# Gate rows leave from a copy turned by TensorE, and the out projection's first weight chunk is split inside the scan's last step

## The chip, the cores and the metric

The kernel runs on one core of one Trainium2 chip. The metric is the device time of one execution in microseconds (us), lower being better. PE is TensorE, DVE is VectorE, ACT is ScalarE, POOL is GpSimd, and SP is SyncE, which here only issues DMAs.

## The reference, cut to what matters

The program computes two blocks one after the other, each two layers deep, on 256 tokens of width 1024, all in float32. The second block works on two streams, the latent tokens (`lat`) and the context tokens (`ctx`). Its layer 0 is what the change touches:

```python
ml = jnp.split(s_lat @ w_ada[i] + b_ada[i], 6, axis=-1)      # shift, scale, gate of the mixer, and of the ff
mc = jnp.split(s_ctx @ w_ada[i] + b_ada[i], 6, axis=-1)
u_lat = modulate(h_lat, g_pre_mix[i], ml[0], ml[1])
...
# even_mixer: the first 512 columns come from an RWKV-7 scan in both directions, the other 512 from attention
out_lat = jnp.concatenate([a_lat, b_lat], axis=-1) @ w_out
...
h_lat = h_lat + ml[2] * rms_norm_2(o_lat, g_post_mix[i])      # ml[2], ml[5], mc[2], mc[5] are the gates
h_lat = h_lat + ml[5] * rms_norm_2(f_lat, g_post_ff[i])
```

The scan keeps a 64x64 state for each of 8 heads: `state = state * w + sa (kk*a) + v k`, `y = state r`, once forward and once in reverse. Before the output product its result `y` is normalised over each head (mean, variance, gain, offset), a bonus is added, and it is multiplied by a gate `g`.

## The kernel before

**Engines and order.** Each engine has one instruction stream, written by hand in the `block` functions at the end of the file. The engines wait for each other through semaphores. PSUM is used as three pools: four banks `acc`, two banks `tr`, two banks `sc`. Every use of a bank is a numbered fill, planned ahead by `stage`. `claim` makes PE wait until the fill before it in that bank is drained, `filled` makes a reader wait until it is written, and `wait_drained` waits for the end of a read.

**Weights.** All weights come in chunks of 1 MB (128 partitions x 2048 floats), which SP loads in one order into four raw slots (`load`, L355). A float32 product is made of three passes of a rounded type: `mm3` (L401 to L403) multiplies high by high, high by low and low by high. So each chunk is split before its use: ACT writes the rounded high part (`ahead_act`, L374), then DVE the rest (`ahead_dve`, L385). The calls of the two functions stand at fixed places in the streams. While `held` is true they don't go on to the chunks of the out projection `out2_0`, since its high slot is memory that the scan still reads.

**The scan.** The scan has `NCH` = 8 steps. In each step two chains run, d = 0 forward and d = 1 in reverse, each over a chunk of 64 tokens. In a step, PE makes the products `nq` into `acc`, which DVE masks (L2103), selects (L2110) and turns (L2111). Five levels (`LEVELS` = 6) of an inverse follow: PE writes `sc`, ACT copies it (L2079), PE multiplies again, and DVE selects (L2122, in the last level L2127) and turns it (L2124). In the same time ACT makes the exponentials of the next step, DVE the products `ar` (`step_ar`) and POOL the products `bk` (L1945). At the end of a step PE makes g, u, the state s and the output y (all at L1978); ACT copies g and u (L2088), DVE updates the state (L2145, L2147) and adds y (L2155, L2158). Nearly all of PE's instructions in the scan are 64x64 matmuls.

The last two steps also carry a part of what comes behind the scan for the first half of the tokens (`rwkv_in_pe`, L2249 and L2254; `y_out_dve`, L2272 to L2276; `y_high_act`, L2280; `y_low_pool`, L2285). POOL's `bonus_pool(1)` (L2214, L2216) comes at the end of the step before the last.

**Behind the scan.** `rwkv_out_dve` splits chunk `out2_0`, then normalises the second half of the tokens: `gn_center_dve` (L2191 to L2194), `gn_var_dve` (L2197, L2198), POOL's power (L2202) and `gn_scale_dve` (L2207), with the split of the next chunk between them. PE's `out2_0_pe` begins with the four products of the first chunk, which holds the rows of the attention half and needs nothing of the normalisation: four token tiles of 4 x 3 matmuls. Ahead of its second chunk it turns the normalised `y` (`y_turned_pe`, L2236).

**The gates.** `ada_gains` (L1134, L1136) puts the gates into `mod_gate`, with the channel on the partitions: a gate row of 1024 channels is 8 columns of 128. The update of h needs a gate row along the free axis in all partitions. So six rows are stored in the DRAM tensor `gate_rows` (`gate_out`, L2347), and come back spread over 128 partitions (`gate_in`, L2355) ahead of the later products. The last of the gates is made by DVE in step 0 of the scan. SP waits for it (`mod_ready`), issues the six stores, then loads the first `out2_0` chunk into the one raw slot which the scan doesn't use, and then waits in `scan_over` for the end of the scan.

Of the kernel before, what the change touches and what calls it, by code (L numbers as in the profile page):

```python
# [16 lines left out]
P = 128  # L17
# [110 lines left out]
def first_and_second_block(nc, I, consts, out):  # L128

    with ExitStack() as ctx:  # L130
# [5 lines left out]
        def sem(name):  # L136
            if name not in made:
                made[name] = ctx.enter_context(nc.semaphore(name))
            return made[name]
# [82 lines left out]
        def stage(key, acc=0, tr=0, sc=0):  # L222
            acc_at[key], tr_at[key], sc_at[key] = fills
            fills[0] += acc
            fills[1] += tr
            fills[2] += sc
# [17 lines left out]
        def filled(eng, pool, f):  # L244

            b, full, _ = POOLS[pool]
            eng.wait_ge(full, f + 1)
            return b[f % len(b)]
# [210 lines left out]
        plan_ada(range(20, 24), lambda n: sc_at["attBc"] + 3 * n)  # L459
        stage("yTB", tr=4)  # L460
        for s in range(NCH):
            stage(("step", s), acc=12, tr=4, sc=4 * (LEVELS - 1))
            if s == NCH - 2:
                stage(("rwkv_turned", 0), tr=2)
            if s >= NCH - 2:
                stage(("rwkv_in", 0, s - (NCH - 2)), sc=2)
# [622 lines left out]


        mod_ready = sem("mod_ready")

        def ada_pe(pe, att, i, n):

# [341 lines left out]
        k_tok = r2.take(4, 256)  # L1436
        rope_t = r2.take(2, 512)
        rate0 = r2.take(4, S2)
        r0 = Region(0)
        rate1 = r0.take(4, S2)  # L1440
        lc0 = r0.take(4, S2)
# [529 lines left out]
        def step_pe(pe, s):  # L1971
# [29 lines left out]
                    ins.then_inc(acc_full, 1)  # L2001
            if first_step:
                yTB_turn(pe, *LATS)
            for lev in range(1, LEVELS):
                for d, q in enumerate(scans):
                    if lev == 1:
                        pe.wait_ge(x_set[d], s + 1)
                    if lev == 1 and first_step:
                        pe.wait_ge(y_cleared, 2)
                    ps = claim(pe, "sc", lev_fill(s, d, lev, 0))  # L2010
                    blocks(ps, HD, lambda j: q.nq[:, j, 0, :], lambda j: q.x[:, j, :]).then_inc(sc_full, 1)
                if lev <= len(TURNS):
                    turn(*TURNS[lev - 1])
                for d, q in enumerate(scans):
                    if lev > 1:
                        pe.wait_ge(xt_set[d], (LEVELS - 2) * s + lev - 1)
                    wait_drained(pe, "sc", lev_fill(s, d, lev, 0))
                    ps = claim(pe, "sc", lev_fill(s, d, lev))
                    if lev < LEVELS - 1:
                        ins = blocks(ps, HD, lambda j: q.xt[:, j, :], lambda j: q.y[:, j, :])  # L2020
                    else:
                        ins = blocks(ps, HD, lambda j: q.y[:, j, :], lambda j: q.xt[:, j, :])
                    ins.then_inc(sc_full, 1)
# [42 lines left out]
        def step_act(act, s):  # L2066
            def keep_turned(d, i):
                q, f = scans[d], turned_fill(s, d, i)
                ps = filled(act, "tr", f)
                act.activation((q.b_tok, q.k_tok)[i], ps[:, 0:4 * CH].rearrange("p (j c) -> p j c", j=4), ACT.Copy).then_inc(drain("tr", f), 1)  # L2070

            if s == 0:
                yTB_act(act, LATS)
                act.wait_ge(y_cleared, 2)
            for lev in range(1, LEVELS):
                for d, q in enumerate(scans):
                    f = lev_fill(s, d, lev, 0)
                    ps = filled(act, "sc", f)
                    act.activation(cols_of(q.y, lev, d), cols_of(ps[:, 0:4 * CH], lev, d), ACT.Copy).then_inc(drain("sc", f), 1)  # L2079
                if lev <= len(TURNS):  # L2080
                    keep_turned(*TURNS[lev - 1])
                if lev == 2 and s + 1 < NCH:
                    for d in range(2):
                        step_exps(act, d, s + 1)
            for what in "gu":
                for d, q in enumerate(scans):
                    f = chain_fill(s, d, what)
                    act.activation((q.g if what == "g" else q.u)[:, :, :], filled(act, "acc", f)[:, 0:4 * CH].rearrange("p (j c) -> p j c", j=4),  # L2088
                                   ACT.Copy).then_inc(drain("acc", f), 1)
                if what == "g" and s == NCH - 2:  # L2090
                    y_affine_act(act, 0)
            if s >= NCH - 2:
                y_high_act(act, 0, s - (NCH - 2))
# [3 lines left out]
        def step_dve(dve, s):  # L2097
# [35 lines left out]
                gn_center_dve(dve, 0)  # L2133
            if s == 5:
                gn_var_dve(dve, 0)
            if s >= NCH - 2:
                y_out_dve(dve, 0, s - (NCH - 2))
            for d, q in enumerate(scans):
# [189 lines left out]
        class Post:  # L2328
# [15 lines left out]
            def gate_out(self, sp):  # L2344

                for i, s in enumerate(self.streams):
                    sp.dma_start(gate_rows[self.rows_before + i].rearrange("(k p) -> p k", p=P),  # L2347
                                 mod_gate[:, self.l, self.w, :, s], allow_slow_non_contiguous=True).then_inc(gates_stored, 16)

            def gate_in(self, sp):  # L2350

# [510 lines left out]
        @block.sync  # L2862
        def _(sp):
            first_sync_dma(sp)
            for g in range(len(chunks)):
                if g == 1:
                    setup_sync_dma(sp)
                if g == RAW:
                    later_sync_dma(sp)
                    t5_sync_dma(sp)  # L2870
                if g == chunk_at["out2_0"]:
                    sp.wait_ge(mod_ready, 2 * DEPTH)
                    for post in posts.values():
                        post.gate_out(sp)
                if g == chunk_at["out2_0"] + 1:
                    scan_over(sp)
                if g == chunk_at["out2_0"] + 2:
                    mix0.gate_in(sp)
                if g == chunk_at["out2_0"] + 4:
                    ff0.gate_in(sp)  # L2880
                if g == chunk_at["out2_1"]:
                    sp.wait_ge(tr_full, tr_at[("norm", ("mix", 1, 0))] + 4)
                    mix1.gate_in(sp)
                if g == chunk_at["ff1_1"]:
                    sp.wait_ge(tr_full, tr_at["proj1"] + 6)
                    ff1.gate_in(sp)
                if g >= RAW:
                    sp.wait_ge(*release[g - RAW])
                load(sp, g)
            ff1.updated(sp)  # L2890
            sp.dma_start(out.rearrange("(t p) d -> p t d", p=P), h_lat[:, :, :]).then_inc(out_stored, 16)
            sp.wait_ge(out_stored, 16)
# [29 lines left out]
        def _(act):  # L2922
# [29 lines left out]
            for s in range(NCH):  # L2952
                step_act(act, s)
            scan_over(act)
            held[0] = False
            rwkv_out_act(act)
            mix0.scalar(act, mod_norms(0, 1)[0])
            norm_scalar(act, ("ff1", 0), *mod_norms(0, 1), squared=1)
# [56 lines left out]
        def _(dve):  # L3015
# [44 lines left out]
            for s in range(NCH):  # L3060
                step_dve(dve, s)
            scan_over(dve)
            held[1] = False
            rwkv_out_dve(dve)
            mix0.vector(dve, mod_norms(0, 1)[0])
            norm_dve(dve, *mod_norms(0, 1), scaled=1)
# [41 lines left out]
```

## Time and profile before

| | |
|---|---|
| Time, median of 3 runs | 2117.55 us (2115.01 to 2122.07) |
| Time of the profiled execution | 2123.59 us |
| Span of its profile | 2121.7 us |
| PE busy | 1942.7 us, 92% |
| DVE busy | 1133.2 us, 53% |
| ACT busy | 868.3 us, 41% |
| POOL busy | 225.2 us, 11% |
| DMA packets under 512 B | 20375 of 237754 |

The span goes from the first to the last instruction of the profiled execution. Times inside it are counted from its start. The scan runs from about 1003 us to 1246 us, and the part behind it up to the next normalisation until about 1304 us.

### The profile page before, as it was taken

How to read it: one execution, taken by the hardware profiler on the slowest of the kernel's cores; microseconds unless marked ns; L12 is line 12 of the kernel's file. 1: busy time of each engine (PE TensorE's matmuls, PEld its weight loads, DVE VectorE, ACT ScalarE, POOL GpSimd, SP SyncE). 2: the span in 40 equal slices, each digit the busy share in tenths (PEclk: the TensorE clock that was granted, in tenths of full speed). 3: DMA queues.
4: the chain of work that ended last, by engine and by line, in shares of the span. 5: the costliest groups of instructions: out<-in, count | busy, mean ns of one | idle time of the engine just before them, and what ended most of it. 6: DMA issues, size and time to landing. Idle time of an engine off the chain costs nothing. (4 is left out here: it accounts for less than half of the span.)

```text
span 2121.7 us, 36817 instructions
## 1 busy us (share of the span) xinstructions
PE 1942.7 (92%) x15695; PEld 1622.1 (76%) x15695; DVE 1133.2 (53%) x1790; ACT 868.3 (41%) x1538; POOL 225.2 (11%) x257
## 2 busy tenths in 40 slices
PE   5997999899799999989699988899999979888998
PEld 4746998685699888756688976778888668677986
DVE  4565675465567555475356555354444545536653
ACT  4344564335456543455122224322223344544532
POOL 1100121020012200102013311020000011000000
PEclk9987999999799999999899999999999989998999
DMA  7584565458456542343600031523233214004653
GB/s 251 179 278 119 161 191 185 141 179 311 124 160 187 184 136 83 107 143 120 22 4 4 4 121 60 121 80 99 80 99 99 80 40 149 30 24 136 183 194 119
DMA packets 237754, 264.53 MB, mean 125 GB/s; under 512 B 20375, under 2 KB 159895, under 8 KB 237208
## 3 DMA queue, kind: packets, MB, share of 16 engines
q1 hardware_dynamic: 228167, 259.23, 40.0%
q10 hardware_dynamic: 9424, 2.95, 0.8%
q8 instruction: 125, 2.05, 0.4%
q14 instruction: 38, 0.30, 0.0%
HBM read 261.07 MB, written 1.09 MB: 124 GB/s over the span
## 5 line engine op out<-in xcount | busy, mean ns | idle before, releaser
L401 PE MATMUL acc<-rounded,rounded 128*128 128x512 f32 (+1 forms) x2552 | 883.6, 346 | 40.3 <-DVE rounded L651 11.0
L402 PE MATMUL acc<-rounded,rounded 128*128 128x512 f32 (+1 forms) x2552 | 877.1, 344 | 0.0
L403 PE MATMUL acc<-rounded,rounded 128*128 128x512 f32 (+1 forms) x2552 | 876.0, 343 | 0.0
L385 DVE TENSOR_TENSOR rounded<-arena,rounded 128x2048 fp32r<-128x2048 f32 (+1 forms) x194 | 435.1, 2246 | 301.6 <-ACT rounded L374 301.5
L401 PEld LDWEIGHTS acc<-rounded,rounded 128*128 128x128 f32 x2552 | 489.1, 192 | 110.3 <-issue 36.0
L403 PEld LDWEIGHTS acc<-rounded,rounded 128*128 128x128 f32 x2552 | 488.7, 191 | 61.3
L402 PEld LDWEIGHTS acc<-rounded,rounded 128*128 128x128 f32 x2552 | 489.6, 192 | 59.4 <-issue 0.2
L374 ACT ACTIVATE rounded<-arena 128x2048 fp32r<-128x2048 f32 (+1 forms) x194 | 362.8, 1872 | 354.6 <-PE acc L403 324.7
L1978 PE MATMUL sc<-arena 64*64 64x64 f32 x2560 | 102.3, 229 | 25.1 <-DVE arena L2111 12.8
L1978 PEld LDWEIGHTS sc<-arena 64*64 64x64 f32 x2560 | 89.9, 141 | 35.7 <-DVE arena L2111 16.1
L1396 DVE SCALAR_TENSOR_TENSOR arena<-acc,pcol,arena 128x254 f32<-128x254 f32 (+1 forms) x176 | 76.8, 478 | 52.3 <-ACT arena L1377 50.8
L821 PEld LDWEIGHTS sc<-arena 128*128 128x128 f32 x592 | 73.0, 196 | 38.0 <-ACT arena L927 20.4
L2496 ACT ACTIVATE arena<-acc 128x512 f32<-128x512 f32 (+1 forms) x64 | 31.3, 490 | 169.5 <-PE acc L403 143.6
L1978 PE MATMUL acc<-arena 64*64 64x64 f32 (+1 forms) x2496 | 94.0, 233 | 5.5 <-issue 4.1
L2510 DVE TENSOR_TENSOR arena<-arena 128x512 f32<-128x512 f32 (+1 forms) x64 | 37.4, 585 | 111.9 <-ACT arena L2496 111.8
L1978 PEld LDWEIGHTS acc<-arena 64*64 64x64 f32 x2496 | 90.3, 138 | 8.2 <-issue 6.4
L821 PE MATMUL sc<-arena 128*128 128x64 f32 (+1 forms) x592 | 82.5, 286 | 7.7 <-ACT arena L927 7.4
L912 ACT ACTIVATE arena<-acc,stat 128x256 f32<-128x256 f32 (+2 forms) x128 | 66.3, 525 | 56.0 <-DVE stat L854 31.2
L1377 ACT ACTIVATE arena<-acc,pcol 128x256 f32<-128x256 f32 x88 | 45.0, 562 | 106.3 <-PE acc L403 106.3
L2079 ACT ACTIVATE arena<-sc 128x128 f32<-128x128 f32 x80 | 22.3, 278 | 139.2 <-PE sc L1978 126.8
L2359 POOL TENSOR_TENSOR stat<-stat,half 128x1 f32<-128x1 f32 x12 | 8.8, 729 | 658.8 <-DVE stat L2474 658.8
L609 PE MATMUL tr<-keep,arena 128*128 128x128 f32 x176 | 31.9, 335 | 46.4 <-DVE arena L600 34.9
(241 smaller groups left out, 1727.8 us busy)
## 6 DMA issues: line engine op xcount, KB each, us to landing
arena<-in_w_ff SPq DMA_DIRECT2D x64, 1024.0 KB, 5.3
arena<-in_w_ada SPq DMA_DIRECT2D x48, 1024.0 KB, 5.2
arena<-in_w_up SPq DMA_DIRECT2D x88, 512.0 KB, 5.0
arena<-in_w_in SPq DMA_DIRECT2D x24, 1024.0 KB, 5.1
arena<-in_w_down SPq DMA_DIRECT2D x20, 1024.0 KB, 5.0
arena<-in_w_out SPq DMA_DIRECT2D x16, 1024.0 KB, 5.1
arena<-in_w_in_even SPq DMA_DIRECT2D x9, 1024.0 KB, 5.3
arena<-in_w_in_odd SPq DMA_DIRECT2D x8, 1024.0 KB, 5.2
```

The lines of the kernel that those rows point to most:

```text
L374: act.activation(r32(high_slot(c)[:, 0:size(c)]), raw_slot(c)[:, 0:size(c)], ACT.Copy).then_inc(high_made, 1)
L385: dve.tensor_tensor(r32(w), w, r32(high_slot(c)[:, 0:size(c)]), ALU.subtract).then_inc(split_made, 1)
L401: pe.matmul(ps, ah, bh, start=first, stop=False)
L402: pe.matmul(ps, ah, bl, start=False, stop=False)
L403: return pe.matmul(ps, al, bh, start=False, stop=last)
L609: ins = pe.transpose(ps[:, k * P:(k + 1) * P], xn[:, tt, kt * P:(kt + 1) * P], ident)
L821: ins = pe.matmul(ps[:, m * e:(m + 1) * e], self.probT[:, u % 2, n * P:(n + 1) * P], x, start=(kb == 0), stop=(kb == self.width(u) // P - 1))
L912: act.activation(self.prob[:, u % 2, m, 0:w], bank("acc", f)[:, 0:w], ACT.Exp, bias=self.neg_max[:, 2 * u + m:2 * u + m + 1], accum_out=se ...
L1377: act.activation(conv[:, i % 2, s, :], ps[:, s * SEQ:(s + 1) * SEQ], ACT.Identity, bias=col("conv_b", l * 2 * FT + s * FT + i), scale=conv ...
L1396: ins = dve.scalar_tensor_tensor(c, ps[:, s * SEQ:(s + 1) * SEQ - back], conv_col(l, j, i, s), c, ALU.mult, ALU.add)
L1978: ins = pe.matmul(out[h], lhsT[h], rhs[h], start=start, stop=stop)
L2510: dve.tensor_tensor(lo, lo, lo, ALU.mult).then_inc(hid_squared, 1)
```

## The change

The six stores no longer read `mod_gate` with its channels on the partitions. In step 1 of the scan PE turns the whole of `mod_gate` (128 partitions x 64 columns) into a `tr` bank with one instruction, ACT copies it to `gate_cols` (64 partitions x 128), and SP, which waits for that copy in place of `mod_ready`, stores eight partitions of 128 floats for each row. A `tr` fill is added for it.

ACT splits the first `out2_0` chunk (high part) at the head of the scan's last step, behind waits for the last readers of the slot, and DVE makes the low part in the same step, behind the last level and ahead of `y_out_dve`. The calls at their old places then find nothing to do.

```diff
@@ the plan of the fills
         for s in range(NCH):
+            if s == 1:
+                stage("gates", tr=1)
             stage(("step", s), acc=12, tr=4, sc=4 * (LEVELS - 1))
@@
+        mod_gates = mod_gate.rearrange("p l w k s -> p (l w k s)")
+        gate_cols = r2.take(P)
@@ step_pe, ahead of the levels
+            if s == 1:
+                pe.wait_ge(mod_ready, 2 * DEPTH)
+                pe.transpose(claim(pe, "tr", tr_at["gates"])[0:mod_gates.shape[1], 0:P], mod_gates, ident).then_inc(tr_full, 1)
@@ step_act, ahead of the levels
+            if s == 1:
+                n = mod_gates.shape[1]
+                act.activation(gate_cols[0:n, :], filled(act, "tr", tr_at["gates"])[0:n, 0:P], ACT.Copy).then_inc(drain("tr", tr_at["gates"]), 1)
+            if s == NCH - 1:
+                for d in range(2):
+                    act.wait_ge(ar_done[d], NCH)
+                    act.wait_ge(bk_done[d], 2 * NCH)
+                act.wait_ge(bonus_in, 2)
+                held[0] = False
+                ahead_act(act, chunk_at["out2_0"])
@@ step_dve, behind the levels
+            if s == NCH - 1:
+                held[1] = False
+                ahead_dve(dve, chunk_at["out2_0"])
             if s >= NCH - 2:
                 y_out_dve(dve, 0, s - (NCH - 2))
@@ gate_out
-                    sp.dma_start(gate_rows[self.rows_before + i].rearrange("(k p) -> p k", p=P),
-                                 mod_gate[:, self.l, self.w, :, s], allow_slow_non_contiguous=True).then_inc(gates_stored, 16)
+                    at = 2 * KT * (2 * self.l + self.w)
+                    sp.dma_start(gate_rows[self.rows_before + i].rearrange("(k p) -> k p", p=P),
+                                 gate_cols[at + s:at + 2 * KT:2, :]).then_inc(gates_stored, 16)
@@ block.sync
                 if g == chunk_at["out2_0"]:
-                    sp.wait_ge(mod_ready, 2 * DEPTH)
+                    wait_drained(sp, "tr", tr_at["gates"])
@@ block.scalar and block.vector, behind scan_over
-            held[0] = False
-            held[1] = False
```

SP's stream around the stores before; `in_w_ada` is the last weight ahead of the scan, `in_w_out` the chunks of `out2_0`:

```order
L355 DMA arena<-in_w_ada 128x4x512 x16
L2347 DMA gate_rows<-mod_gate 128x8x1 x6
L355 DMA arena<-in_w_out 128x4x512 x2
L2355 DMA arena<-gate_rows 128x2048
L355 DMA arena<-in_w_out 128x4x512 x2
```

The same place of the change:

```order
L355 DMA arena<-in_w_ada 128x4x512 x16
L2368 DMA gate_rows<-arena 8x128 x6
L355 DMA arena<-in_w_out 128x4x512 x2
L2376 DMA arena<-gate_rows 128x2048
L355 DMA arena<-in_w_out 128x4x512 x2
```

The order is the same; a store now has 8 rows of 128 floats as its source where it had 128 partitions of 8 single floats. The source shown as `arena` is `gate_cols`.

ACT's stream in the scan's last step before, from the end of the step ahead of it (L2088, the copies of g and u) over the five levels (L2079, L2070) to the split of the first chunks (L374):

```order
L2088 ACTIVATE arena<-acc 128x4x64 x2
L2280 ACTIVATE rounded_51<-arena 128x2x256
L2079 ACTIVATE arena<-sc 128x64x2 x2
...
L2079 ACTIVATE arena<-sc 128x4x32 x2
L2088 ACTIVATE arena<-acc 128x256
L2088 ACTIVATE arena<-acc 128x4x64 x3
L2280 ACTIVATE rounded_51<-arena 128x2x256
L374 ACTIVATE rounded_64<-arena 128x2048
L374 ACTIVATE rounded_65<-arena 128x2048
```

The same place of the change, where L2105, L2300, L2096 are the lines that were L2088, L2280, L2079:

```order
L2105 ACTIVATE arena<-acc 128x4x64 x2
L2300 ACTIVATE rounded_51<-arena 128x2x256
L374 ACTIVATE rounded_64<-arena 128x2048
L2096 ACTIVATE arena<-sc 128x64x2 x2
...
L2096 ACTIVATE arena<-sc 128x4x32 x2
L2105 ACTIVATE arena<-acc 128x256
L2105 ACTIVATE arena<-acc 128x4x64 x3
L2300 ACTIVATE rounded_51<-arena 128x2x256
L374 ACTIVATE rounded_65<-arena 128x2048
```

One L374 has moved from behind the step to ahead of its first level.

DVE's stream at the end of the last step before, from the last selects (L2127) over `y_out_dve`, the state and y to the split (L385) and the normalisation (L2191 on):

```order
L2127 COPY_PREDICATED arena<-pairs,sc 128x4x32 x2
L2272 TENSOR_TENSOR arena<-sc,arena 128x2x256
L2275 TENSOR_TENSOR arena<-arena 128x2x256
L2276 TENSOR_TENSOR arena<-arena,sc 128x2x256
L2145 TENSOR_TENSOR arena<-acc,arena 128x256
L2147 TENSOR_TENSOR arena<-arena,stat 128x256
L2145 TENSOR_TENSOR arena<-acc,arena 128x4x64
L2147 TENSOR_TENSOR arena<-arena,stat 128x256
L2158 TENSOR_TENSOR arena<-arena,acc 128x4x64 x2
L385 TENSOR_TENSOR rounded_69<-arena,rounded_64 128x2048
L2191 TENSOR_REDUCE stat<-arena 128x4x4
```

The same place of the change, with L2144 for L2127, L2292 to L2296 for L2272 to L2276, L2165 to L2178 for L2145 to L2158, and L2211 for L2191:

```order
L2144 COPY_PREDICATED arena<-pairs,sc 128x4x32 x2
L385 TENSOR_TENSOR rounded_69<-arena,rounded_64 128x2048
L2292 TENSOR_TENSOR arena<-sc,arena 128x2x256
L2295 TENSOR_TENSOR arena<-arena 128x2x256
L2296 TENSOR_TENSOR arena<-arena,sc 128x2x256
L2165 TENSOR_TENSOR arena<-acc,arena 128x256
L2167 TENSOR_TENSOR arena<-arena,stat 128x256
L2165 TENSOR_TENSOR arena<-acc,arena 128x4x64
L2167 TENSOR_TENSOR arena<-arena,stat 128x256
L2178 TENSOR_TENSOR arena<-arena,acc 128x4x64 x2
L2211 TENSOR_REDUCE stat<-arena 128x4x4
```

The L385 has moved from ahead of the normalisation to ahead of `y_out_dve`.

## Rows read from the trace of the kernel before

**Rows 1.** Timeline of DVE, steps 0 to 2 (start, length, line, operation, idle time before)

```profile
1006.08 1.27 DVE L2103 TENSOR_TENSOR arena<-acc,keep 128x512 f32<-128x512 f32 x2
...
1040.29 0.30 DVE L2127 COPY_PREDICATED arena<-pairs,sc 128x128 f32<-128x128 uint8 x1 [1.59 <-PE sc L1978]
...
1052.16 0.69 DVE L2103 TENSOR_TENSOR arena<-acc,keep 128x512 f32<-128x512 f32 x1 [0.51 <-PE acc L1978]
...
1069.62 0.51 DVE L2127 COPY_PREDICATED arena<-pairs,sc 128x128 f32<-128x128 uint8 x2
...
1078.60 0.69 DVE L2103 TENSOR_TENSOR arena<-acc,keep 128x512 f32<-128x512 f32 x1 [0.45 <-PE acc L1978]
```

**Rows 2.** Timeline of SP, from the stores to behind the scan

```profile
1012.10 10.01 SPq L2347 DMA_DIRECT2D gate_rows<-mod_gate  x6
1022.15 224.18 SPq L355 DMA_DIRECT2D arena<-in_w_out  x2
```

**Rows 3.** Timeline of PE in step 0, two of its gaps

```profile
1021.61 1.12 PE L1978 MATMUL sc<-arena 64*64 64x64 f32 x16 [5.22 <-DVE arena L2122]
...
1046.33 8.41 PE L1978 MATMUL acc<-arena 64*64 64x64 f32 x172 [2.37 <-issue]
```

**Rows 4.** DMA queues from 1012 to 1046 us: packets, MB, share of 16 engines

```profile
DMA packets 6771, 1.12 MB, mean 33 GB/s; under 512 B 6256, under 2 KB 6256, under 8 KB 6768
...
q8 instruction: 3, 0.05, 1.8%
```

**Rows 5.** The same from 1050 to 1076 us

```profile
q8 instruction: 5, 0.08, 1.3%
```

**Rows 6.** Windows: PE, PEld, DVE, ACT, POOL busy (instructions), PE clock, DMA share, GB/s

```profile
1022.00:1030.00 8.00, 6.45 (x121) 5.79 (x119) 1.50 (x5) 0.94 (x3) 0.00 (x0) 0.67 1.94 3
...
1240.00:1250.50 10.50, 5.11 (x168) 4.86 (x164) 5.63 (x9) 3.00 (x4) 1.27 (x1) 0.94 0.35 115
1250.50:1256.00 5.50, 5.39 (x13) 4.27 (x14) 5.33 (x7) 1.91 (x1) 0.24 (x1) 0.50 1.01 398
1256.00:1264.30 8.30, 8.30 (x37) 6.49 (x35) 3.10 (x2) 0.00 (x0) 4.64 (x1) 1.00 0.58 227
```

**Rows 7.** Timeline of PE, end of the scan and first `out2_0` chunk

```profile
1240.45 4.88 PE L1978 MATMUL acc<-arena 64*64 64x64 f32 x160 [0.22 <-ACT arena L2088]
...
1250.61 0.77 PE L401 MATMUL acc<-rounded,rounded 128*128 128x512 f32 x1 [5.29 <-DVE rounded L385]
...
1264.41 2.08 PE L2236 MATMUL tr<-keep,arena 64*64 64x64 f32 x64
```

**Rows 8.** Timeline of ACT, last step and behind it

```profile
1221.10 0.28 ACT L2079 ACTIVATE arena<-sc 128x128 f32<-128x128 f32 x1 [8.78 <-PE sc L1978]
...
1250.96 1.91 ACT L374 ACTIVATE rounded<-arena 128x2048 fp32r<-128x2048 f32 x1 [3.02 <-DMA arena<-in_w_out]
```

**Rows 9.** Timeline of DVE, last step and behind it

```profile
1235.39 0.30 DVE L2127 COPY_PREDICATED arena<-pairs,sc 128x128 f32<-128x128 uint8 x1 [0.37 <-PE sc L1978]
1238.32 0.69 DVE L2272 TENSOR_TENSOR arena<-sc,arena 128x512 f32<-128x512 f32 x1 [2.62 <-PE sc L2249]
...
1245.37 0.42 DVE L2158 TENSOR_TENSOR arena<-arena,acc 128x256 f32<-128x256 f32 x1 [0.98 <-PE acc L1978]
...
1250.27 1.21 DVE L2191 TENSOR_REDUCE stat<-arena 128x16 f32<-128x1024 f32 x1
...
1255.59 2.28 DVE L385 TENSOR_TENSOR rounded<-arena,rounded 128x2048 fp32r<-128x2048 f32 x1
1260.68 1.23 DVE L2207 TENSOR_TENSOR arena<-arena,stat 128x1024 f32<-128x1024 f32 x1 [2.80 <-POOL stat L2202]
```

**Rows 10.** Timeline of POOL: both L2202 and the last bonus instruction

```profile
1180.31 2.94 POOL L2202 TENSOR_TENSOR stat<-stat,half 128x16 f32<-128x16 f32 x1
...
1214.25 2.42 POOL L2216 TENSOR_TENSOR arena<-arena 128x1024 f32<-128x1024 f32 x1
...
1255.76 4.88 POOL L2202 TENSOR_TENSOR stat<-stat,half 128x16 f32<-128x16 f32 x1 [13.24 <-DVE stat L2198]
```

## The prediction

> **What bounds the kernel now.** The page says that PE is busy for 92% of the span, so a change has to be looked for where PE is not busy, or slow. Two such places lie around the edits. I read them in this order: the timeline of DVE for the length of each scan step, PE's and SP's timelines and the DMA queues for what is different in a long one, and the timelines of all engines at the end of the scan for what ends last there.
>
> *Step 0 of the scan is far too long.* The first L2103 of a step marks its start. Step 1 runs from 1052.16 to 1078.60, 26.44 us. Step 0 runs from 1006.08 to 1052.16, 46.08 us [rows 1]. The last level's selects come 34.2 us after the start in step 0, and 17.5 us in step 1. From them to the next step it is 11.9 us against 9.0 [rows 1]. So the delay begins inside the levels and has not quite ended behind them. SP issues the six gate stores from 1012.10 on, and the load of the first `out2_0` chunk at 1022 [rows 2]. PE has six gaps between 1016 and 1046 us, of which the first was 5.22 us, and the last, 2.37 us, is put down to "issue", which means that no semaphore was late [rows 3]. In the same 34 us the queues moved 6256 packets under 512 B, about the 6 x 1024 single floats of the stores, and only three blocks of the queue that brings instructions; its share of 1.8% is 0.018 x 16 x 34 = 9.8 engine-us, 3.3 us for a block [rows 4]. In step 1 five blocks came in 26 us, at 0.013 x 16 x 26 / 5 = 1.1 us each [rows 5]. A DMA share of 1.94 with 3 GB/s, at a PE clock of 0.67 [rows 6], is the picture of queues that are stopped up by small packets, and of a PE that is starved by them and then loses its clock.
>
> *Behind the scan PE waits.* Its last scan matmul ends at 1240.45 + 4.88 = 1245.33, and the first product of `out2_0` starts at 1250.61, released by DVE's split [rows 7]. The granted clock is then 0.50 for 5.5 us, in which 13 matmuls take 5.39 us; at full clock 37, two of them in part, take 8.30 us [rows 6]. That is 0.415 and 0.234 us for each. PE comes to `y_turned_pe` at 1264.41 [rows 7]. DVE's scaling of y had been done at 1260.68 + 1.23 = 1261.91 [rows 9], so there PE itself came last.
>
> **The change part by part.**
>
> *The stores, removed from step 0.* How long would step 0 be without them? Step 1 has 26.44 us. Step 0 lacks the products with the state, 32 matmuls in g and 32 in y: at 4.88 us for 160 of that kind [rows 7], 64 x 0.0305 = 2.0 us. That leaves 24.5 us, and 46.1 - 24.5 = 21.6 us are lost now. If the missing matmuls shorten nothing, 19.6 us are lost.
>
> What comes back? The new stores are 6 x 8 = 48 pieces of 512 B, with nothing of the sort in the trace; by count they are 1/128 of what they replace, and 24 KB are 0.1 us at the 398 GB/s of the window at 1250.50 [rows 6]. I take 0. The load of the chunk (1 MB) now falls into step 1 alone. It was in flight at the last of the gaps, 2.37 us, when the small packets were nearly through; that is the upper bound, and 0 the lower one. Where 5 MB were loaded at 398 GB/s PE ran 13 of 13 matmuls without a gap [rows 6], though with far fewer instructions per us. I take 0.8 us.
>
> The Trainium skill, "Runtime: NRT & Kernel Launch", section "Instruction fetch mechanics", says that each sequencer brings its program in blocks of 256 instructions through a DMA queue of its own, and that crossing a block is mostly hidden. The blocks of 16 KB are in the trace (0.05 MB for three), but step 0 shows them not hidden. By the rule alone nothing would be won here, and the sum would be 7 us instead of 28.
>
> *The turning of the gates, added to step 1.* One PE instruction of 128 columns: 64 matmuls of 64 columns take 2.08 us [rows 7], so 0.03 to 0.1 us; it stands ahead of the first level, where PE anyway waits for DVE's turn after its first product. The wait on `mod_ready` is met since step 0. ACT's copy is like an L2079, 0.28 us, and ACT sits idle for 8.78 us ahead of the first level of the last step [rows 8], as it does in step 1. If that cover were gone, 0.3 us. SP goes on a step later than before; its chunk load is needed only at the end of the scan, some 150 us later. I take 0.1 us for all.
>
> *The split, moved into the last step.* ACT: L374 takes 1.91 us [rows 8] and waits for POOL's second bonus instruction, done at 1214.25 + 2.42 = 1216.67 [rows 10]. So it ends at 1218.6, and the first level's copy is due at 1221.10 [rows 8]: 2.5 us to spare. Behind it in ACT's queue stand all level copies, for which PE waits; this is the cover to watch. DVE: L385 takes 2.28 us and starts at 1235.39 + 0.30 = 1235.69, ends at 1237.97, and `y_out_dve` starts at 1238.32, released by PE [rows 9]: 0.35 us to spare. If that is gone, the state update shifts by the same few tenths, and I count nothing.
>
> *What PE gets.* It starts `out2_0` at 1245.4. The clock was at full rate in the scan, and 0.94 on the mean over the window that holds the idle time [rows 6]; with no idle time I take full clock from the start. The 48 matmuls take 48 x 0.234 = 11.2 us, until 1256.6. If the clock fell anyway, 13 x 0.18 = 2.4 us more.
>
> *What is late next.* The normalisation. DVE is through with the scan at 1245.37 + 0.42 = 1245.79 and no longer has a split ahead of it. From L2191 to the next L385 it is 1250.27 to 1255.59, 5.3 us [rows 9], so POOL's power starts at 1251.2; it took 2.94 us once and 4.88 us when an L385 had begun just before it [rows 10]. It ends at 1254.1 to 1256.1. DVE meanwhile splits the second chunk. Its landing doesn't move, since SP loads it behind the scan: ACT's high part still ends at 1252.87 [rows 8], DVE's low part at 1255.2. The scaling (1.23 us) ends between 1256.4 and 1257.4. So PE, done at 1256.6, turns y between 1256.7 and 1257.5. I take 1257.2, and the gain is 1264.41 - 1257.2 = 7.2 us, with 5.0 as the lower bound (the clock falls) and 7.7 as the upper one.
>
> The Trainium skill, "SBUF — State Buffer", section "SBUF: two separate sides", says that a port pair shared by DVE and GpSimd is locked for a whole instruction by whoever starts first. The two lengths of L2202 agree with that. By the rule POOL, starting first now, would hold the second L385 back until 1254.1, and y would be scaled by 1257.7, a gain of 6.7 us.
>
> From the turning of y on, all that follows (bonus, gate, second chunk, update) hangs on PE, and chunks and gate rows were in the slots long before. I see nothing absolute in it, so the shift goes to the end.
>
> *Sum.* 21.6 - 0.8 - 0.1 + 7.2 = 27.9 us. The profiled execution took 2123.59 us (its span 2121.7 us), and would take 2095.7 us. It was 6.0 us above the median of 2117.55; the median less 27.9 is 2089.7 us, and I say 2090.
>
> **The rivals.**
>
> *Only the out projection gains.* The stall of step 0 would come from something else than the single floats: from the chunk load, or from writing to `gate_rows` at all. It would then move to step 1 at full size. For it speaks that the gaps go on until 1046 us [rows 3], with the chunk in flight. Against it, that the first and longest gap, 5.22 us, came before SP had issued the load at 1022 [rows 2, 3]. Time: 2117.55 - 7.2 = 2110.
>
> *Only the stores gain.* POOL's bonus comes late and ACT's split holds up the first level, or the normalisation takes all that PE wins. The first decides once the bonus ends over 2.5 us later against the step than now; each further us costs one. Time: 2117.55 - 20.7 = 2097.
>
> *Slower.* The stall moves to step 1 and grows there: SP issues stores and load at one blow, ahead of a step that needs more instructions than step 0. It must grow from 21.6 to over 21.6 + 7.2 + 6.4 = 35.2 us before the kernel is slower by more than 0.3%; then 2124 or more. Only 48 packets would have to do this, and nothing in the profile speaks for it.
>
> *The change does nothing*: the stall was an effect of profiling, which records each packet. The profiled execution is only 6.0 us above the median, so at least 15 of the 21.6 us are there without it too. At 15 the time is 2096, inside the range.
>
> **How the numbers follow.** Both gains as worked out: 0.84, with terms of 15 to 21.6 for the stores and 5.0 to 7.7 for the projection, less up to 2.4, and 2 us for the median: 2084 to 2100. Only the stores: 0.06, inside it too. Only the projection: 0.08, half of it faster by over 0.3% (6.4 us), half within. Slower 0.02. A range of 2083 to 2100 leaves out about 2 in 10 with its edges. A measurement of this kernel can tell about 0.3% from no change. Faster 0.94, same 0.04, slower 0.02.
>
> **What would show it.** In the profile after, the first L2103 (its new line) of steps 0 and 1 stand 24 to 25 us apart, with at most one gap of up to 2.4 us in step 1; packets under 512 B are fewer by 6144; PE goes on into the projection with a gap under 0.3 us and no clock of 0.50; from the last matmul of the scan to the turning of y it is 11 to 12.5 us, 19.1 now. Wrong would be a step 1 of over 35 us, a first level copy in the last step later than 4 us after DVE's first turn, or a normalisation that ends later than 12.5 us after the scan.

## The result, and the profile after

| | before | after |
|---|---|---|
| Median | 2116.28 us (4 runs, 2113.93 to 2122.07) | 2090.68 us (4 runs, 2084.78 to 2093.34) |
| Profiled execution, its span | 2123.59 us, 2121.7 us | 2088.72 us, 2086.9 us |
| DMA packets under 512 B | 20375 | 14182 |

The ratio is 0.9856, with a 95% interval of 0.9829 to 0.9883: 1.4% faster. The forecast was 2090.

The page's line on packets, after:

```profile
DMA packets 231610, 264.54 MB, mean 127 GB/s; under 512 B 14182, under 2 KB 153750, under 8 KB 231063
```

There are 6193 fewer packets under 512 B than before, about the six times 1024 floats of the old stores.

**Step 0.** Timeline of DVE after, steps 0 and 1 (answers to [rows 1]):

```profile
1001.98 1.27 DVE L2120 TENSOR_TENSOR arena<-acc,keep 128x512 f32<-128x512 f32 x2
...
1026.64 0.69 DVE L2120 TENSOR_TENSOR arena<-acc,keep 128x512 f32<-128x512 f32 x1 [0.45 <-PE acc L1982]
...
1053.41 0.69 DVE L2120 TENSOR_TENSOR arena<-acc,keep 128x512 f32<-128x512 f32 x1 [0.45 <-PE acc L1982]
```

Timeline of SP after (answers to [rows 2]):

```profile
1029.79 3.93 SPq L2368 DMA_DIRECT2D gate_rows<-arena  x6
1033.76 188.49 SPq L355 DMA_DIRECT2D arena<-in_w_out  x2
```

Step 0 now lasts 1026.64 - 1001.98 = 24.66 us instead of 46.08. Step 1, which holds the new stores and the chunk load, lasts 26.77 us instead of 26.44. The other steps up to the last but one are as before within 0.1 us.

**The last step.** Timeline of ACT after (answers to [rows 8]), where the bracket holds the idle time ahead of the row:

```profile
1191.64 1.91 ACT L374 ACTIVATE rounded<-arena 128x2048 fp32r<-128x2048 f32 x1 [4.62 <-POOL arena L2236]
...
1195.80 0.29 ACT L2096 ACTIVATE arena<-sc 128x128 f32<-128x128 f32 x1 [2.25 <-PE sc L1982]
```

ACT's split waits for POOL's bonus, as worked out, and ACT is then idle for 2.25 us until PE's first product of the level is there. So the split doesn't hold up the level.

Timeline of DVE after, around the split and behind the scan (answers to [rows 9]):

```profile
1211.52 2.28 DVE L385 TENSOR_TENSOR rounded<-arena,rounded 128x2048 fp32r<-128x2048 f32 x1
...
1214.24 0.69 DVE L2292 TENSOR_TENSOR arena<-sc,arena 128x512 f32<-128x512 f32 x1 [0.44 <-PE sc L2269]
...
1221.99 1.22 DVE L2211 TENSOR_REDUCE stat<-arena 128x16 f32<-128x1024 f32 x1 [0.28 <-DVE arena L2178]
...
1229.03 2.29 DVE L385 TENSOR_TENSOR rounded<-arena,rounded 128x2048 fp32r<-128x2048 f32 x1 [1.62 <-ACT rounded L374]
1231.24 1.22 DVE L2227 TENSOR_TENSOR arena<-arena,stat 128x1024 f32<-128x1024 f32 x1
```

Timeline of POOL after (answers to [rows 10]):

```profile
1227.49 2.91 POOL L2222 TENSOR_TENSOR stat<-stat,half 128x16 f32<-128x16 f32 x1 [9.05 <-DVE stat L2218]
```

Timeline of PE after, end of the scan (answers to [rows 7]):

```profile
1216.37 4.88 PE L1982 MATMUL acc<-arena 64*64 64x64 f32 x160 [0.22 <-ACT arena L2105]
1221.18 0.50 PE L401 MATMUL acc<-rounded,rounded 128*128 128x512 f32 x1
...
1232.72 2.08 PE L2256 MATMUL tr<-keep,arena 64*64 64x64 f32 x64
```

Windows after, columns as in [rows 6], one in the last step and two in the projection:

```profile
1196.00:1202.00 6.00, 4.66 (x98) 4.52 (x100) 2.75 (x7) 1.04 (x4) 0.00 (x0) 0.72 0.01 3
...
1221.20:1226.70 5.50, 5.50 (x26) 4.44 (x25) 4.99 (x6) 0.00 (x0) 0.00 (x0) 1.00 0.68 232
1226.70:1232.60 5.90, 5.90 (x26) 4.45 (x24) 4.11 (x4) 1.92 (x1) 2.91 (x1) 1.00 1.02 398
```

PE goes from the scan's last matmul into the first product without a gap, and the granted clock is 1.00 in both windows of the projection. From the end of the scan's last matmul, 1221.25, to the turning of y it is 11.47 us instead of 19.08. DVE's scaling ends at 1231.24 + 1.22 = 1232.46 and PE's last product of the chunk at 1232.6: both arrive together.

**Where the time went.** The profiled spans differ by 34.8 us. From the first L2103 to the turning of y it was 1264.41 - 1006.08 = 258.33 us, and is 1232.72 - 1001.98 = 230.74 us: 27.6 us less, and this is the part that the change touches. Ahead of the scan the execution was 1006.08 - 1001.98 = 4.1 us shorter, and behind the turning 3.1 us; both lie outside the edits, and the runs of either kernel differ by over 8 us among themselves.

### The profile page after: what moved, and what is told of

The parts are those of the page before. It is cut to its first block and busy times, and to the rows that moved or that the text cites. A ratio compares the mean times of both kernels' runs of the same rounds, so it can differ in the third digit from the quotient of the medians.

```text
span 2086.9 us, 36823 instructions
## 1 busy us (share of the span) xinstructions
PE 1930.2 (92%) x15696; PEld 1612.7 (77%) x15696; DVE 1132.6 (54%) x1790; ACT 868.3 (42%) x1539; POOL 223.4 (11%) x257
## 2 busy tenths in 40 slices
DMA packets 231610, 264.54 MB, mean 127 GB/s; under 512 B 14182, under 2 KB 153750, under 8 KB 231063
## 5 line engine op out<-in xcount | busy, mean ns | idle before, releaser
L385 DVE TENSOR_TENSOR rounded<-arena,rounded 128x2048 fp32r<-128x2048 f32 (+1 forms) x194 | 435.0, 2246 | 298.6 <-ACT rounded L374 298.5
L374 ACT ACTIVATE rounded<-arena 128x2048 fp32r<-128x2048 f32 (+1 forms) x194 | 362.8, 1872 | 357.8 <-PE acc L403 321.0
L2438 DVE TENSOR_TENSOR arena<-arena,acc 128x512 f32<-128x512 f32 x56 | 37.9, 685 | 67.2 <-PE acc L403 67.2
```

The source lines that it names most:

```text
L374: act.activation(r32(high_slot(c)[:, 0:size(c)]), raw_slot(c)[:, 0:size(c)], ACT.Copy).then_inc(high_made, 1)
L385: dve.tensor_tensor(r32(w), w, r32(high_slot(c)[:, 0:size(c)]), ALU.subtract).then_inc(split_made, 1)
L2438: ins = dve.tensor_tensor(o, o, ps[:, :], ALU.add)
```

## The experiments

Kernels whose name speaks of floats, loads or bytes make extra transfers into memory that nothing reads; `late_split_pe_busy` makes products that nothing uses.

### gates_alone

The change, with the split left behind the scan:

```diff
-            if s == NCH - 1:      # step_act: the waits, held[0] = False, ahead_act(...)
-            if s == NCH - 1:      # step_dve: held[1] = False, ahead_dve(...)
             scan_over(act)
+            held[0] = False
             scan_over(dve)
+            held[1] = False
```

> The gates' half of the change, with the split back behind the scan. My theory: step 0 of the scan (first L2103-like instruction of step 0 to that of step 1) is as in the change, 24.7 us instead of 46.1, and behind the scan nothing is won: PE waits 5.3 us, 13 matmuls run at half clock, and from the last scan matmul to the turning of y it is 19.1 us as before. Time 21 us below the kernel before, about 2095. Rival (the two halves are not independent, the split pays for a part of the stores' gain): a time below 2092 or above 2101.

Measured: 2095.93 us median beside 2117.66, ratio 0.9896 (0.987 to 0.9923). Step 0 lasts 24.66 us. The end of the scan is as it was, and the turning of y comes 18.52 us behind it.

Timeline of PE in this kernel, first product behind the scan:

```profile
1222.57 0.77 PE L401 MATMUL acc<-rounded,rounded 128*128 128x512 f32 x1 [5.37 <-DVE rounded L385]
```

So the stores alone give 21.7 us by the medians.

### split_alone

The kernel before, with the split moved and the stores as they were:

```diff
@@ step_act, ahead of the levels; step_dve, ahead of y_out_dve
+            if s == NCH - 1:      # the waits, held[0] = False, ahead_act(...)
+            if s == NCH - 1:      # held[1] = False, ahead_dve(...)
```

> The split's half of the change, with the single-float stores as before. My theory: step 0 stays at 46 us, from the last scan matmul to the turning of y 11.5 us instead of 19.1; time 7.6 us below the kernel before, about 2108.5. Rival (the shorter end only shows because the chunk and the gates come later): over 14 us from the last scan matmul to the turning of y, and less than 4 us won.

Measured: 2110.48 us beside 2117.66, ratio 0.996 (0.9944 to 0.9976). Step 0 is still long, 43.46 us, and the end of the scan is that of the change.

Timeline of PE in this kernel, end of the scan:

```profile
1236.98 4.88 PE L1978 MATMUL acc<-arena 64*64 64x64 f32 x160 [0.22 <-ACT arena L2095]
1241.80 0.50 PE L401 MATMUL acc<-rounded,rounded 128*128 128x512 f32 x1
...
1253.37 2.08 PE L2246 MATMUL tr<-keep,arena 64*64 64x64 f32 x64
```

The scan ends at 1241.86, and y is turned 11.51 us later. The split alone gives 7.2 us by the medians. The two halves add up within their intervals: 0.9896 + 0.996 - 1 = 0.9856, the ratio of the change.

### stores_in_step3

Is it the stores that hold step 0 up, or what else happens there? The kernel before, with the old stores held back until step 3, while the chunk load stays in step 0:

```diff
                 if g == chunk_at["out2_0"]:
                     sp.wait_ge(mod_ready, 2 * DEPTH)
-                    for post in posts.values():
-                        post.gate_out(sp)
                 if g == chunk_at["out2_0"] + 1:
+                    sp.wait_ge(acc_full, nq_fill(3, 0, 0) + 1)
+                    for post in posts.values():
+                        post.gate_out(sp)
                     scan_over(sp)
```

> The kernel before with the six single-float stores held back to step 3 of the scan; the chunk's load stays in step 0, now without them. My theory (the stores stop up the queues that bring instructions): step 0 takes 24.7 to 27 us, and step 3 takes 20 us more than the 26.4 of its neighbours, with three or four instruction blocks in 34 us. Rival (the chunk load, or the start of the scan, is the cause): step 0 stays above 40 us and step 3 stays at 26 to 28.

Measured (one run): 2115.44 us. The steps 0 to 4 last 25.94, 27.21, 26.43, 41.06 and 27.92 us; step 3 lasts 26.49 in the kernel before.

Timeline of SP in this kernel:

```profile
1012.35 0.38 SPq L355 DMA_DIRECT2D arena<-in_w_out  x1
1085.91 8.93 SPq L2347 DMA_DIRECT2D gate_rows<-mod_gate  x6
```

DMA queues of this kernel in step 3, 1085 to 1127 us:

```profile
DMA packets 6247, 0.13 MB, mean 3 GB/s; under 512 B 6240, under 2 KB 6240, under 8 KB 6240
...
q1 hardware_dynamic: 6240, 0.02, 51.8%
q8 instruction: 6, 0.10, 1.8%
```

The stall goes where the stores go, and costs 41.06 - 26.49 = 14.6 us there; 20 us were expected. The chunk load without them costs 25.94 - 24.66 = 1.3 us in step 0 and 27.21 - 26.44 = 0.8 us in step 1. So the stores are the cause and the load isn't. That 14.6 + 2.1 is less than the 21.4 us of the kernel before could come from the load being queued behind the stores; but the stall also differs between kernels that have both, 21.4 us before and 43.46 - 24.66 = 18.8 us in `split_alone`.

### late_split_pe_busy

How much of the 7 us is the wait, and how much the clock that falls in it? `gates_alone`, with five float32 products of 128x512 that PE makes while it would wait for the split. ACT reads one column of the result, behind its second split, so that the bank comes free:

```diff
+            ps = claim(pe, "tr", tr_at["warm"])
+            for i in range(5):
+                ins = pe.matmul(ps[:, :], ident, keep[:, 0:512], start=True, stop=True)
+            ins.then_inc(tr_full, 1)
             tok_gemm(pe, "out2_0"
...
```

> The gates' half alone, and PE runs five plain float32 products of 512 columns (their result isn't used) while it would wait for the late split. The split is as late as before, so only the clock differs. Theory: the 48 matmuls of the first chunk all run at 0.234 us, 11.2 us, and from the last scan matmul to the turning of y it is 16.5 us: 2.4 of the 7.6 us are the clock's, 5.2 the wait's. Rival (the clock falls for another reason than the idle time): a granted clock of 0.50 for some 5 us as before, and 19 us.

Measured (one run): 2099.46 us. The scan ends at 1224.29.

Windows of this kernel, from its first product behind the scan on:

```profile
1229.40:1235.00 5.60, 5.60 (x24) 4.54 (x25) 5.43 (x7) 1.97 (x2) 0.27 (x1) 1.00 1.00 394
```

Windows of `gates_alone`, the same stretch of its work:

```profile
1222.50:1228.00 5.50, 5.43 (x16) 4.35 (x17) 5.33 (x7) 1.91 (x1) 0.37 (x1) 0.64 1.02 401
```

Timeline of PE in `late_split_pe_busy`, the turning of y:

```profile
1241.13 2.08 PE L2247 MATMUL tr<-keep,arena 64*64 64x64 f32 x64 [0.28 <-DVE arena L2218]
```

The clock stays full, and the turning of y comes 16.84 us behind the scan: 1.7 us less than in `gates_alone`, 2.2 less than before, and 5.4 more than in the change. So about 2 of the 7 us are the clock's, and the other 5 are the wait for DVE's split. The bracket shows that here DVE's scaling is what comes last, 0.28 us behind PE.

### two_float_rows and six_float_rows

From here on the changed kernel is the base, whose step 0 lasts 24.66 us. SP issues extra transfers in step 0, behind `mod_ready` and ahead of everything that it issues otherwise. First two rows of the old form, then all six:

```diff
+                    sp.wait_ge(mod_ready, 2 * DEPTH)
+                    for i in range(2):          # six_float_rows: range(6)
+                        sp.dma_start(spare[i].rearrange("(k p) -> p k", p=P), mod_gate[:, 0, i, :, 0],
+                                     allow_slow_non_contiguous=True).then_inc(spare_stored, 16)
                     wait_drained(sp, "tr", tr_at["gates"])
```

> The changed kernel plus two further rows stored as 1024 single floats each into a DRAM tensor that nothing reads, issued where the kernel before issued its six. Alone in a step, six such rows cost 14.6 us (41.06 against 26.49). If the cost goes by the count, step 0 takes 24.66 + 4.9 = 29.5 us. Rival (what an engine has fetched ahead covers a short stop): step 0 under 26 us.

> The control for the others of this kind: the changed kernel plus all six rows as 1024 adjacent single floats each, into a DRAM tensor that nothing reads, at the place in step 0. Two such rows made step 0 30.16 us long instead of 24.66. If the price is per row, 24.66 + 3 x 5.5 = 41 us; with the 14.6 us seen in step 3, 39 us. Rival (the price is paid once, for the first rows): 30 to 33 us.

Measured (one run each): 2092.1 us, with a step 0 of 30.16 us, 5.5 more than the base; and 2109.48 us, with a step 0 of 42.01 us, 17.35 more.

Timeline of PE in `two_float_rows`:

```profile
1014.69 1.12 PE L1985 MATMUL sc<-arena 64*64 64x64 f32 x16 [4.16 <-issue]
```

DMA queues of `six_float_rows`, 1005 to 1025 us:

```profile
DMA packets 5007, 0.05 MB, mean 3 GB/s; under 512 B 5005, under 2 KB 5005, under 8 KB 5005
...
q1 hardware_dynamic: 5005, 0.02, 64.6%
q8 instruction: 2, 0.03, 1.5%
```

Two rows make one gap of 4.16 us in which no semaphore is late, and six rows several. In 20 us only two blocks of instructions came, at 0.015 x 16 x 20 / 2 = 2.4 us each. The stores need nothing else of the change to do harm, and their price is 2.8 to 2.9 us for each row of 1024 floats.

Does PE stand because its instructions are late? DMA queues of `two_float_rows`, from 1007.5 to 1008.5 us:

```profile
q8 instruction: 1, 0.02, 23.4%
```

And from 1008.5 to 1015 us:

```profile
DMA packets 65, 0.00 MB, mean 0 GB/s; under 512 B 65, under 2 KB 65, under 8 KB 65
...
q1 hardware_dynamic: 65, 0.00, 0.6%
```

The block that starts in the first stretch takes 0.234 x 16 x 1 = 3.7 us, long beside 1.1 us in a quiet step. But it has landed by 1012.3 at the latest, and hardly a packet of the stores starts after 1008.5. PE nevertheless stands from 1010.53 to 1014.69. So a slow block goes with the gap, and it isn't shown that the block is what ends it. That few blocks come in a stall doesn't show it either, since engines that stand still need few.

### float_rows_spread, rows_of_64_bytes, float_loads

Is it the number of packets? Three kernels with the same 6 x 1024 pieces: single floats, each 512 B from the next in DRAM; pieces of 64 B, 512 B apart; and single floats that are loaded instead of stored.

```diff
+                        sp.dma_start(spare[i].rearrange("(k p) b -> p k b", p=P)[:, :, 0:1], mod_gate[...]      # spare [6, D, 128]
+                        sp.dma_start(spare[i].rearrange("(k p) b -> p k b", p=P)[:, :, 0:16], keep[...]         # the same, 64 B
+                        sp.dma_start(spare_sb[:, KT * i:KT * (i + 1)], I["w_ada_2"][...].rearrange("(k p) -> p k", p=P)
```

> The changed kernel plus six rows of 1024 single floats into a DRAM tensor that nothing reads, each float at the head of a 512-byte row of its own, so that no two touch the same stretch of DRAM. If the number of packets makes the stop, step 0 takes 24.66 + 14.6 = 39 us. Rival (neighbouring 4-byte writes from several DMA engines hold each other up): step 0 under 30 us.

> As float_rows_spread, but each of the 6144 pieces has 64 bytes. If the number of packets below 512 bytes makes the stop, 39 us or a little more for step 0. Rival (it is the 4 bytes): step 0 under 30 us.

> The changed kernel plus six DMAs of 1024 single floats each in the other direction, from DRAM into an SBUF tile that nothing reads, at the same place. If the number of packets makes the stop, 39 us for step 0. Rival (it is the writing to DRAM): step 0 under 28 us.

Measured (one run each), times and lengths of step 0: 2099.44 us and 25.16; 2092.38 and 24.66; 2097.01 and 24.65.

DMA queues of `float_rows_spread`, 1005 to 1025 us:

```profile
DMA packets 6244, 0.09 MB, mean 5 GB/s; under 512 B 6240, under 2 KB 6240, under 8 KB 6240
...
q1 hardware_dynamic: 6240, 0.02, 17.1%
q8 instruction: 4, 0.07, 1.3%
```

The same count of packets of the same size costs 0.5 us instead of 17.35, or nothing. All 6240 are through in these 20 us with 17.1% of the engines, and four blocks of instructions come beside them. So the count theory falls, and the theory that small packets as such do it falls too. The times in all differ by more than step 0 does, since the scan starts at 1000.24 to 1006.22 us in these and the next kernels and its step 6 lasts 30.2 or 31.2 us; the length of step 0 is the measure.

### floats_64_bytes_apart, adjacent_64_bytes, floats_by_partition

What is left is where in DRAM the floats lie. Single floats 64 B apart; pieces of 64 B that adjoin; and single floats 8 B apart, where the eight floats of a partition share 64 B. In the last one, writers of the same 64 B read the same partition, which in the old stores they don't.

```diff
+ ... spare[i].rearrange("(k p) b -> p k b", p=P)[:, :, 0:1]            # floats_64_bytes_apart, spare [6, D, 16]
+ ... spare[i].rearrange("(k p b) -> p k b", p=P, b=16)                 # adjacent_64_bytes, spare [6, 16 * D]
+ ... spare[i].rearrange("(p k b) -> p k b", p=P, b=2)[:, :, 0:1]       # floats_by_partition, spare [6, 2 * D]
```

> As six_float_rows, with the single floats 64 bytes apart. The floats 512 bytes apart cost 0.5 us. If what counts is that several DMA engines write into the same few dozen bytes at once, step 0 stays under 26 us here too. Rival (the stretch in which writes get in each other's way is larger than 64 bytes): over 30 us.

> 6 x 1024 pieces of 64 bytes as in rows_of_64_bytes, which cost nothing, but adjacent in DRAM instead of 512 bytes apart. If adjacent pieces collide only when they share less than 64 bytes, step 0 stays under 26 us. Rival (any small adjacent pieces collide): over 30 us.

> As six_float_rows, but the eight floats of one partition lie together (8 bytes apart, 64 bytes for each partition), so that neighbouring floats are written by the same DMA engine one after the other. If the stop comes from several engines in the same few dozen bytes, step 0 stays under 26 us. Rival (small writes into one stretch are slow whoever makes them): over 30 us.

Measured (one run each), times and lengths of step 0: 2096.45 us and 25.05; 2090.2 and 24.65; 2113.27 and 44.26.

DMA queues of `floats_by_partition`, 1005 to 1025 us:

```profile
DMA packets 5258, 0.05 MB, mean 3 GB/s; under 512 B 5256, under 2 KB 5256, under 8 KB 5256
...
q1 hardware_dynamic: 5256, 0.02, 91.0%
q8 instruction: 2, 0.03, 0.9%
```

Waits of the same kernel, 1012 to 1046 us (engine, tile and line, released by, us in all, times, longest):

```profile
POOL arena L1952 <- remote: 20.8, 1, 20.8
DVE arena L2142 <- remote: 20.1, 3, 9.9
ACT arena L2099 <- remote: 14.7, 3, 7.4
```

Single floats are harmless once each has 64 B of its own (0.4 us), and adjoining pieces are harmless once each is 64 B long. Floats that share 64 B cost 19.6 us even where all of them come from one partition. That speaks against my guess that it needs several DMA engines writing to the same place, and for the rival, that small writes into one stretch of DRAM are slow whoever makes them; no view here shows which DMA engine took which float. DVE, ACT and POOL all wait for something that the profile doesn't place in this core's engines ("remote"). I read that as the same stall as "issue" on PE: in `two_float_rows` DVE's idle time of 4.07 us ends at 1014.35, and PE's of 4.16 us at 1014.69.

## Why the prediction was right, and where it wasn't

- **Step 0, 21.6 us forecast.** It was 21.4 us in the profiles (46.08 - 24.66), 21.7 us by the medians of `gates_alone`. This is the price of the stores and the load behind them together; the same stores by themselves cost 14.6 us in step 3, and six such rows 17.35 us in step 0. The length of a natural step 0 was forecast as 24.5 us from step 1 less its 64 matmuls, and was 24.66.
- **The mechanism of the stall.** The place holds: the stall went with the stores into step 3. The way through the instruction queue is argued and not shown: a block takes 3.7 us beside the stores of `two_float_rows`, but PE stands on after that block has landed. The step "queues that are stopped up by small packets" was too wide. `float_rows_spread`, `rows_of_64_bytes`, `float_loads` and `adjacent_64_bytes` put as many packets under 512 B through the same queue for 0 to 0.5 us. In its place: writes of 4 B that lie 4 or 8 B apart in DRAM, so that 8 or 16 share 64 B; 64 B apart they cost 0.4 us. The estimate for the new stores, 0, was argued from the packet count; it was right, but the count isn't what makes it right, since 6144 pieces of 64 B cost nothing either.
- **The chunk load and the gates' turning in step 1, 0.9 us forecast.** Step 1 grew by 0.33 us. With the same stores and load in it, it lasted 26.44 us in `gates_alone`, as before the change, and 27.03 in seven other kernels, so the term is 0 to 0.6 us and was put too high. In `stores_in_step3` the load cost 2.1 us in steps 0 and 1; all this is inside the bounds of 0 to 2.4 us.
- **The split in the last step, nothing forecast.** ACT has 2.25 us to spare ahead of the level copy (2.5 forecast), and DVE 0.44 us ahead of `y_out_dve` (0.35 forecast). From the last step's first L2120, 1192.24, to its last selects, 1211.32, it was 19.08 us instead of 17.86. The split doesn't bring these 1.2 us by itself: `split_alone` and seven of the eight kernels with extra transfers, which all hold it, took 17.85 to 17.89 us there, as the kernels without it did. The changed kernel (19.08) and `float_loads` (19.07) are the exceptions, and in the changed one the window from 1196 us has a granted clock of 0.72, where the same stretch of `split_alone` has 1.00. Step 6 likewise lasts 30.2 us in seven of the fourteen kernels and 31.2 in the others, with the split and without. So I put down what is lost there to falls of the clock. Each kernel has one profile, and a fall in the last step came in two of ten profiles with the split and in none of four without; that the split has no part in it isn't shown.
- **The out projection, 7.2 us forecast.** The profiles gave 7.6 us (19.08 to 11.47), `split_alone` 7.6 us in the profile and 7.2 by the medians. The worked chain held: the normalisation is late next, POOL's power took 2.91 us, where 2.94 to 4.88 had been allowed, and the scaling ended at 11.2 us behind the scan, with PE 0.2 us later. The second L385 didn't come ahead of the power, since it had to wait 1.62 us for ACT's high part. The prediction also worked out that POOL, starting first, would hold this L385 back until its power ends, for a gain of 6.7 us. The trace doesn't agree: L385 starts at 1229.03, as soon as ACT is done, 1.37 us ahead of the end of the power at 1230.40, and takes its usual 2.29 us. Only the other half of that rule shows here, a power that takes 4.88 us when L385 has begun just before it. The clock's part, forecast as 2.4 us if it fell, was 1.7 to 2.2 us in `late_split_pe_busy`.
- **The rivals.** "Only the out projection gains" needed the chunk load or any write to `gate_rows` as the cause: `stores_in_step3` and `gates_alone` rule it out. "Only the stores gain" is ruled out by `split_alone`. "Slower" would have shown a step 1 of over 35 us; it was 26.77. "An effect of profiling" is ruled out by the medians of runs without a profile, 21.7 us in `gates_alone`.
- **The sum, 27.9 us forecast.** The touched part shrank by 27.6 us. That this is so close is in part luck: 0.6 us too much for step 1 and 0.4 us too little for the projection make up for most of the 1.2 us of the last step. By the medians the change gained 25.6 us. The ends of the range don't follow from its terms, which give 2117.55 - 21.6 - 7.7 - 2 = 2086 and 2117.55 - 15 - 5.0 + 2.4 + 2 = 2102 where 2084 and 2100 were said; the measured 2090.68 lies inside both.

Open: whether pieces of 8 to 32 B that adjoin are slow too, and floats 16 or 32 B apart; whether it is the shared 64 B that counts or how densely a larger stretch is written; whether the memory or the DMA engine is what makes such writes slow; what it is that PE lacks in its gaps; and how the old stores and the load behind them share the 21.4 us. The likely answer to the last lies between 1.4 us (18.8 less the 17.35 of `six_float_rows`) and 6.8 us (21.4 less 14.6) for the load. The kernel before shows that the load takes part. DMA queues from 1036 to 1042 us, where no packet of the stores starts any more:

```profile
DMA packets 121, 0.25 MB, mean 41 GB/s; under 512 B 0, under 2 KB 0, under 8 KB 121
...
q1 hardware_dynamic: 121, 0.25, 76.2%
```

A packet of 2 KB takes 0.762 x 16 x 6 / 121 = 0.60 us there, and PE's last gap ends at 1046.33 [rows 3].

## What to carry to other kernels

Look for a step that is longer than its like, and for waits called "issue" or "remote" on several engines at once: they point at something outside the engines' own work, and the DMA queues of the same stretch name the suspect, which moving it to another step then tests. When a column is stored as a row of DRAM, turn it on PE first, or give each piece 64 B of its own; how the pieces lie in the destination counts there, not their number, nor their size alone. A split that the next stage waits for costs its own length and also the clock that PE loses meanwhile; it goes where both engines are idle inside the loop, and the next late arrival (here the normalisation, 0.2 us behind PE) says how much is left to win.

## What the runs showed of the hardware

- 6144 single floats stored so that 16 share 64 B cost the scan 14.6 us in step 3 and 17.4 us in step 0, and with 8 in 64 B 19.6 us, though no engine waits for the data. The same floats 64 or 512 B apart cost 0.4 and 0.5 us; pieces of 64 B and loads of single floats cost nothing.
- The profile counts instruction blocks as packets of a queue on the DMA engines. A block took 1.1 us in a quiet step [rows 5], 3.3 us under the old stores [rows 4], and two rows of 1024 floats were enough for a gap of 4.16 us on PE. The Trainium skill, "Runtime: NRT & Kernel Launch", section "Instruction fetch mechanics", says that crossing a block is mostly hidden. The trace of the kernel before agrees in steps 1 to 7, where PE has no gap over 0.3 us that is put down to "issue"; in step 0 it has five, of 0.89 to 2.37 us, and whether the blocks are their cause isn't shown.
- A transfer of 1 MB at up to some 400 GB/s in step 1, with the new stores ahead of it, cost the scan 0 to 0.6 us; 24 KB in single floats cost 17.35 us.
- A DVE instruction on two operands in SBUF (L385) that began inside a POOL power took 2.29 us, as it does alone, in the changed kernel and in `split_alone`; a power that began inside L385 took 4.88 us instead of 2.91.
